# The last transposes of nine attentions, issued inside the output projection instead of ahead of it

## What is computed

```python
def memory_cross_attention(x, mem_k, mem_v, w_q, w_o):
    q = (x @ w_q).reshape(bsz, s, X_HEADS, X_HEAD_DIM)
    sc = jnp.einsum('bshd,bmhd->bhsm', q, mem_k).astype(jnp.float32) * (X_HEAD_DIM ** -0.5)
    p = jax.nn.softmax(sc, axis=-1)
    o = jnp.einsum('bhsm,bmhd->bshd', p.astype(mem_v.dtype), mem_v).reshape(bsz, s, D_MODEL)
    return o @ w_o
```

## Time and profile before

| | before |
|---|---|
| device time, median of 3 runs | 2838.77 us (2836.06 to 2847.71) |
| device time of the profiled execution | 2849.37 us |
| its span, first to last instruction | 2847.6 us |
| mean granted TensorE clock | 0.959 of full speed |
| PE busy | 2655.3 us (93%) |
| PE weight load busy | 2506.9 us (88%) |
| POOL busy | 1820.0 us (64%) |
| ACT busy | 1453.0 us (51%) |
| DVE busy | 1123.6 us (39%) |

### The profile page before, as it was taken

How to read it: one execution, slowest core, us unless ns; L and a number is a source line. 1 busy time by engine, 2 the same in 40 slices (tenths; PEclk the granted TensorE clock), 3 DMA queues, 4 the chain that set the end, 5 groups by cost and what they waited for, 6 DMA issues and landing times.

```text
span 2847.6 us, 52622 instructions
## 1 busy us (share of the span) xinstructions
PE 2655.3 (93%) x19848; PEld 2506.9 (88%) x19848; DVE 1123.6 (39%) x2658; ACT 1453.0 (51%) x2564; POOL 1820.0 (64%) x770
## 2 busy tenths in 40 slices
PE   7899899999989999988999997999999899989998
PEld 6787679999978799987889997899978899978998
DVE  5216634111144631135343366333433433463434
ACT  5226644444444554444555565555645555455655
POOL 0437647878855778863568865488645588635786
PEclk8999999999999999999999998999979999989999
DMA  6225434555533555542345543355423355423454
GB/s 240 99 75 172 143 101 158 181 176 187 184 121 136 169 174 180 183 141 90 119 141 183 180 148 103 119 178 184 155 89 115 123 182 180 140 73 114 164 183 141
DMA packets 115637, 421.75 MB, mean 148 GB/s; under 512 B 12832, under 2 KB 14112, under 8 KB 114976
## 3 DMA queue, kind: packets, MB, share of 16 engines
q1 hardware_dynamic: 115200, 417.00, 43.9%
q10 hardware_dynamic: 288, 2.62, 0.2%
HBM read 418.52 MB, written 1.05 MB: 147 GB/s over the span
## 4 chain that ended last, share of the span: by engine, by line
PE 59%; issue 18%; POOL 15%; DVE 5%; ACT 3%; DMA 1%; POOLq 0%; DVEq 0%; SPq 0%; ACTq 0%
POOL ring_low L2250 15%; PE bank L594 10%; PE bank L595 10%; PE bank L600 10%; PE bank L585 7%; PE bank L586 7%; PE bank L587 7%; PE bank L860 2%; PE bank L889 2%; PE bank L742 1%; ACT scr L1302 1%; DMA ring<-in_units 1%; PE bank L907 1%; DVE scr L1698 1%; DVE xt L2155 0%
## 5 line engine op out<-in xcount | busy, mean ns | idle before, releaser
L2250 POOL TENSOR_TENSOR ring_low<-ring,ring_high 128x1024 fp32r<-128x1024 f32 x766 | 1819.8, 2405 | 1009.7 <-ACT ring_high L1178 799.3
L594 PE MATMUL bank<-high,ring_high 128*128 128x256 f32 (+1 forms) x3372 | 859.5, 291 | 10.5 <-ACT vt L1214 8.5
L595 PE MATMUL bank<-low,ring_high 128*128 128x256 f32 (+1 forms) x3372 | 852.2, 288 | 0.0
L594 PEld LDWEIGHTS bank<-high,ring_high 128*128 128x128 f32 x3372 | 649.2, 193 | 18.2 <-issue 8.6
L595 PEld LDWEIGHTS bank<-low,ring_high 128*128 128x128 f32 x3372 | 649.2, 193 | 6.8
L1410 ACT ACTIVATE ring_high<-ring 128x1024 fp32r<-128x1024 f32 x448 | 466.2, 1053 | 83.2 <-DMA ring<-in_units 83.2
L600 PE MATMUL bank<-high,ring_low 128*128 128x256 f32 (+1 forms) x3372 | 491.9, 288 | 0.0
L600 PEld LDWEIGHTS bank<-high,ring_low 128*128 128x128 f32 x3372 | 445.6, 192 | 5.6
L1178 ACT ACTIVATE ring_high<-ring 128x1024 fp32r<-128x1024 f32 x337 | 351.6, 1054 | 124.5 <-DMA ring<-in_units 123.7
L585 PE MATMUL bank<-hid_high,ring_high 128*128 128x256 f32 x1232 | 349.3, 284 | 11.1 <-DVE hid_low L1980 9.0
L586 PE MATMUL bank<-hid_low,ring_high 128*128 128x256 f32 x1232 | 348.6, 283 | 0.0
(11 more groups left out here) (220 smaller groups left out, 3391.5 us busy)
## 6 DMA issues: line engine op xcount, KB each, us to landing
ring<-in_units SPq DMA_DIRECT2D x785, 512.0 KB, 3.3
xt<-in_x SPq DMA_DIRECT2D x2, 1024.0 KB, 9.3
nbias<-in_bias ACTq DMA_DIRECT2D x1, 1536.0 KB, 7.8
vt<-in_mem ACTq DMA_DIRECT2D x1, 1024.0 KB, 6.8
out_x<-xt SPq DMA_DIRECT2D x8, 128.0 KB, 1.7
consts<-in_consts SPq DMA_DIRECT2D x1, 832.0 KB, 9.8
cols<-in_cols SPq DMA_DIRECT2D x1, 639.0 KB, 6.5
consts<-in_consts SPq DMA_DIRECT2D x1, 512.0 KB, 7.3
```

Of the source, the lines that this page charges most:

```text
L594: first = pe.matmul(out, w[0], x[0], start=start, stop=False)
L595: pe.matmul(out, w[0], x[1], start=False, stop=False)
L2250: pool.tensor_tensor(whole(ring_low, u), whole(ring, u), whole(ring_high, u).bitcast(fp32), ALU.subtract).then_inc(unit_ready, 1)
```

## The change

`project` gets an argument `between`, a pair of a block number and a function; the function is called in the opening just ahead of that block and of its wait. `attention` on the PE no longer calls `out_t(last)`; it returns the last item's first block and `out_t(last)` as such a pair, and each of the nine attentions hands it to the projection behind it. With that `fill(5 * last + 5)` comes ahead of `out_t(last)`. ACT, DVE, POOL and SP keep their code. The projection of the recurrent mixer gets `None`.

```diff
--- before.py
+++ after.py
@@ -599,7 +599,7 @@
 
                     return pe.matmul(out, w[1], x[0], start=False, stop=stop)
 
-                def project(st, u0, n_tiles, src, n, depth=KD, ready=None, base=0, per_unit=1, after=None):
+                def project(st, u0, n_tiles, src, n, depth=KD, ready=None, base=0, per_unit=1, after=None, between=None):
 
                     width = P * per_unit
                     opened = 0
@@ -607,6 +607,8 @@
 
                         opened = min(3, n_tiles)
                         for k in range(depth):
+                            if between and k == between[0]:
+                                between[1]()
                             pe.wait_ge(*when(*ready(k)))
                             for m in range(opened):
                                 if k == 0:
@@ -941,8 +943,8 @@
                         fill(5 * s + 2)
                         values(s)
                         fill(5 * s + 4)
-                    out_t(last)
                     fill(5 * last + 5)
+                    return items[last]["tiles"][0], lambda: out_t(last)
 
                 def ffn(name, src, ready):
 
@@ -1049,9 +1051,9 @@
                 project_v("ab", UNITS["ab"] + 16, 4, tokens(0, 2 * T), 4)
 
                 ab_needs = [("ab", "rope", m) for m in ROT0] + [("ab", "out", 15), ("ab", "vout", 15)]
-                attention("at0", steps_at0(), ab_needs, ada=ADA0)
+                ending = attention("at0", steps_at0(), ab_needs, ada=ADA0)
                 project("ab_out", UNITS["ab_out"], 8, split(0, 2 * T), 2 * T,
-                        ready=lambda k: ("sub", "done", 2 + k // 2) if k < 4 else ("at0", "o", 8 + k),
+                        ready=lambda k: ("sub", "done", 2 + k // 2) if k < 4 else ("at0", "o", 8 + k), between=ending,
                         after=stats_summed("f0", n=2 * T))
                 ffn("ffn_x0", split(0), lambda k: ("f00", "h", k))
                 ffn("ffn_c0", split(1), lambda k: ("f01", "h", k))
@@ -1073,8 +1075,8 @@
                 rotate("c_q", 7)
                 c_needs = ([("c_q", "rope", m) for m in range(8)]
                            + [("c_k", "rope", 1), ("c_v", "vout", 3)])
-                attention("at1", gqa_items(512, band_masks, False, COLS["sinks_c"]), c_needs, ada=ADA1)
-                project("c_out", UNITS["c_out"], 8, split(0), T, ready=lambda k: ("at1", "o", k),
+                ending = attention("at1", gqa_items(512, band_masks, False, COLS["sinks_c"]), c_needs, ada=ADA1)
+                project("c_out", UNITS["c_out"], 8, split(0), T, ready=lambda k: ("at1", "o", k), between=ending,
                         after=stats_summed("f10"))
                 ffn("ffn_x1", split(0), lambda k: ("f10", "h", k))
 
@@ -1096,7 +1098,7 @@
                         rotate(st + "q", 7)
                         needs = ([(st + "q", "rope", m) for m in range(8)]
                                  + [(st + "k", "rope", 1), (st + "v", "vout", 1)])
-                        attention(st + "t", gqa_items(256, swa_masks, True, COLS["sinks_a"] + 16 * (l // 3)), needs)
+                        ending = attention(st + "t", gqa_items(256, swa_masks, True, COLS["sinks_a"] + 16 * (l // 3)), needs)
                         attended = lambda k, st=st: (st + "t", "o", k)
                     elif kind == 1:
                         st = f"b{l}"
@@ -1152,15 +1154,16 @@
                             reader[n] = (st, "vout", n)
                         needs = ([(st + "uq", "rope", 8 + m) for m in range(4)]
                                  + [(st + "d", "rope", 5), (st + "uq", "out", 7), (st + "uk", "out", 7), (st, "vout", 3)])
-                        attention(st + "t", mla_items(), needs)
+                        ending = attention(st + "t", mla_items(), needs)
                         attended = lambda k, st=st: (st + "t", "o", k // 2)
                     project(st + "o", UNITS[st + "_out"], 8, split(0), T, ready=attended,
+                            between=None if kind == 1 else ending,
                             after=stats_tokens(f"ln{l}0", xin))
                     project(f"x{l}q", UNITS[f"x{l}_q"], 8, split(0), T, ready=lambda k, l=l: (f"ln{l}0", "x", k))
                     mem_needs = [(f"x{l}q", "out", 7)] + ([("mem", "out", 7), ("mem", "vout", 7)] if l == 0 else [])
-                    attention(f"x{l}t", mem_items(), mem_needs)
+                    ending = attention(f"x{l}t", mem_items(), mem_needs)
                     project(f"x{l}o", UNITS[f"x{l}_out"], 8, split(0), T,
-                            ready=lambda k, l=l: (f"x{l}t", "o", k // 2),
+                            ready=lambda k, l=l: (f"x{l}t", "o", k // 2), between=ending,
                             after=stats_tokens(f"ln{l}1", xin))
                     ffn(f"f{l}", split(0), lambda k, l=l: (f"ln{l}1", "x", k))
                     stats_ffn(f"ln{l}2", xin)
```

## The result

The changed kernel takes 2846.39 us (median of 20 runs, 2836.89 to 2859.49), the kernel before 2839.09 (median of 20, 2829.24 to 2850.50). The ratio is 1.0027, with a 95% interval of 1.0014 to 1.0039: 7.7 us slower, between 4 and 11. The forecast was +6 us, 2845, in a range that goes from 2837 to 2853. The change is slower, but by a quarter of a percent: only many runs of both kernels tell it from no change. The prediction took 0.5% as the least that can be told.

The account below looks back on a forecast made before the run. PE, busy 93% of the span, was taken as the bound. New stalls 16.4 + POOL 0.4 - heads 9.4 - tails 0.7 = +6.7 us; 0.7 off for the clock leaves +6: 2838.77 + 6 = 2845 us, range 2837 to 2853.

Parts of the forecast that it names:

- The exchange of waits: At nine attention ends, the exposed wait for normalising is given up for a new one for the split inside the opening.
- nine waits for the low part: PE waits in the projections' openings: about 1.7 us with four transposes, 1.2 with two, near 14 us in total.
- The chain from the first transpose on: In the opening, first transpose to DVE's subtraction plus 0.15 us step to PE: 2.13 or 1.43 us, sum 16.4.
- The head: Projection directly behind the values: 1.33 us saved per cross attention, 0.85 per grouped-query, 9.4 in all; hidden tails 0.7 more.
- `at1`: Attention end with nothing saved before the projection; it pays 1.43 us inside the opening and 0.4 us for POOL.
- the POOL term: Tile 3 of the projection in `at1`: POOL's low part of the fourth unit comes late, 0.4 us lost.
- What stands behind ACT and DVE: Fourth unit's feed and POOL's low part: slack 1.5 us in cross attentions, 0.2 in grouped-query, 0.4 lost in `at1`.
- The feed rival: ACT or POOL reach the fourth unit 1 us later in eight places, tile 3 waits: +14 us, 2853; chance 10%.
- the clock rival: New gaps in the nine openings each bring a half-clock stretch, 15 us on top: 2860 us; chance 9%.
- The half-clock stretch at the head of `at0`: Clock 0.64 over 3 us directly behind `at0`; its loss of 1.7 us might go, 0.7 us taken as gain.
- The head rival: Splitting hides behind something unseen and only the savings ahead of the projections stay: -10.1 us, 2828.7; chance 11%.

Follow-up runs that it names:

- the second measurement: The changed kernel timed once more, 12 runs beside 29 of the kernel before: 2845.11 us, ratio 1.0021 (1.0005 to 1.0037).
- the fourth experiment, feed first: The changed kernel with ACT feeding the projection's fourth unit ahead of its copy of the last item: 2846.97 us.
- copy twice: The changed kernel with ACT's copy of the last item made twice, one after the other: 2849.5 us.
- both versions of block 2: The changed kernel with last transposes ahead of block 2 in all nine attentions (2834.14 us), or all but `at1`, which keeps the old order (2833.66 us).
- the old head: Kernel before (2839.09 us), and the same with last transposes and last conditioning transposes swapped in `at0` and `at1` (2839.16 us).
- the versions with cover: The changed kernel with last transposes earlier: one block earlier (2836.66 us), ahead of block 1 (2837.96), block 2 (2834.14), or block 2 except in `at1` (2833.66).
- the last one: The changed kernel with last transposes ahead of block 2 except in `at1`, which keeps the old order: 2833.66 us, ratio 0.9972 to the kernel before.

## Why the prediction was right

**The exchange of waits** is shown. The forecast named nine waits for the low part, about 1.7 us with four transposes and 1.2 with two, near 14 us in total. They are nine, at 1.41 and 0.93, 10.8 in total. The chain from the first transpose on was put at 2.13 and 1.43 us and measures 2.01 and 1.31. In the sum, 16.4 us become 5 x 2.01 + 4 x 1.31 = 15.3. Most of this is the step from DVE to the PE: I took 0.15 us from the transposes that waited for the normalising, and ahead of line 585 it is 1437.05 - 1436.99 = 0.06. The waits came out shorter than 1.7 and 1.2 for one more reason, which is no time saved: I subtracted 0.38 us for the transposes from the chain, and the profile counts the wait from the modelled end of the last of them, 0.60 us after the first: 2.01 - 0.60 = 1.41.

**The restart** is a term that the forecast had at nothing. Behind each new wait the first matmul is followed after 0.22 us instead of 0.12, 0.9 us in the nine places.

**The head** came out larger than worked in the cross attentions. Before, the distance holds 12.40 - (12.93 - 2.01) = 1.48 us of head, less this restart; the saving itself is 1.58, and the forecast had 1.33 + 0.04. The 0.04 is a misreading: a value matmul there lasts 0.38 us in the trace, not 0.28, so the starts are (1.24 - 0.38)/4 = 0.22 apart and the tail that a seamless joint hides is 0.16. That leaves 0.1 us unexplained. In the grouped-query ones it is 11.28 - (11.67 - 1.31) = 0.92, with the restart 1.02, as the forecast had it (0.85 + 0.17). So a cross attention loses 0.53 us where 0.76 was worked out, a grouped-query one 0.39 against 0.41.

**`at1`** was the costly one, as forecast: nothing is saved at its head, and it loses 1.41 to 1.44 us behind the conditioning transposes and 0.19 for POOL, against 1.43 + 0.41. Without the clock the nine places add up to 4 x 0.53 + 0.49 (`m2t`) + 2 x 0.39 + 1.43 + 0.19 + 0.27 = 5.3 us, against 6.7 in the forecast. The last term is `at0`, where 0.25 was worked out; it is 24.54 - 24.27, from two profiles whose half-clock stretches do not fall on the same matmuls, so it is rough. That 6.7 comes so near is in part luck: the chain was put 1.1 us too high and the POOL term 0.2, the restart 0.9 too low, and the heads 1.1 too small. Both sums lie in the measured interval of 4 to 11. The 5.3, less what the clock gives back in some executions, is near its lower end, and the second measurement gave 1.4 to 10.5. Whether the rest of the measured 7.7 is chance or something outside these places, the times can't tell; the profiles show nothing outside that is longer with the change. That +6 lies within 2 us of it is therefore no proof of the sum; the waits in the trace are.

**What stands behind ACT and DVE** was worked out well enough: slack everywhere but in `at1`. The feed rival fell with the fourth experiment.

**The clock.** In three profiles with the change's own gaps (the change, its second profile, the feed first) there are 27 gaps of 0.93 or 1.41 us inside the opening, and behind none of them did the clock fall; so the clock rival did not happen. It can happen, though: with gaps of 2.04 us a stretch at 1.2 GHz followed once in five. In the Trainium skill (TensorE: Matmul & The Clock Gate, HAM oscillation — how this bites in real kernels) waits of 3 to 5 us between bursts make each next burst cold. No gap in these nine places is that long, so whether the trace agrees at that length no run here shows. Behind the 27 shorter gaps the clock stayed up, and the one fall behind 2.04 us shows that a shorter wait than those can be enough.

The half-clock stretch at the head of `at0` did go in the profiled execution of the change: the clock is 1.00 over the whole distance. Its row from 377 to 380 us, to be set beside the first of the earlier trace rows:

```profile
377.00:380.00 3.00, 3.00 (x15) 2.49 (x14) 0.00 (x0) 0.00 (x0) 0.00 (x0) 1.00 0.00 0
```

It is not gone for good. With the projection directly behind the values, the stretch stands at this place in four profiles (copy twice, feed first, and both versions of block 2; 0.52 from 372 to 375 with the feed first) and is absent in five; with the old head it stands in both. What it is worth is seen in `at0`'s column: 24.54 with the stretch and 23.02 without it, 1.5 us for the same order of the PE. The forecast took 0.7 of its 1.7 us as the likely gain. That was a guess; five profiles of nine would give 0.8, but so few do not fix the share.

**The head rival** failed as argued: the block needs exactly what was just transposed. It becomes true in the versions with cover, and their gain (8 us by the distances, 8 by the ratio of the last one) is near what that rival priced (10.1), less the PE's own time for the transposes, 28 of them at 0.11 us.

## What to carry to other kernels

Moving a step to "just ahead of its use" moves it off one wait and onto the next: count the whole chain from the step to its user, across every engine, and put the step at least that far ahead. When a result passes through two engines on its way back, look for the stretch of independent work that covers the part ahead of the step and the part behind it; here 18 matmuls on one side and 36 to 45 on the other removed both waits in every trace, and a loss of 6 to 8 us became a gain of 4 to 8. A sum of a few us in a kernel of 2840 is checked in the trace, wait by wait, and not by one time. And a step that already sits in some other wait for free, as in `at1`, may be left there, but look for the next wait behind it: there it was worth only 0.15 us in the trace.

## What was not expected of the hardware

The step from one engine to the next depends on what starts: behind DVE's end the first fp32 transpose started after 0.15 us, the first matmul of the split product after 0.06. Behind each gap the first matmul lasts 0.38 instead of 0.28 us and the second comes 0.22 later instead of 0.12, so a gap costs 0.1 us more than its length. A delay too short for the list of waits costs that too, as the row at 1350.97 shows. And a single gap of 2.04 us, in 7.6 us of dense matmuls at 1.00 before it, was once enough to be followed by 3.4 us at 1.2 GHz, where 15 gaps of 1.41 us were not.
